# Contracting over 128 rows instead of 64 or 16 in the mixer of a two-layer decoder

## The chip, the cores and the metric

The kernel runs on one core of one Trainium2 chip. The metric is the device time of one execution in microseconds, as the median of several runs; lower is better.

## What is computed

Two decoder layers over 528 tokens (16 learned meta tokens ahead of 512) of width 1024. Each layer is a SwiGLU feed-forward network, a mixer, and a second feed-forward network, each added to a scaled residual and normalized:

```
x <- LN1(alpha*x + 0.5*SwiGLU_1(x))
x <- LN2(alpha*x + W_out [Pool(u_pool) ; GLA(q,k,v,r,g)])
x <- LN3(alpha*x + 0.5*SwiGLU_2(x))
where [u_pool | q | k | v | r | g_lowrank] = x @ W_in
```

The change is in GLA, gated linear attention with 4 heads, keys of 64 and values of 128 per head:

```
def step(S, xs):                       # one chunk of tokens, one head
    b = cumsum(gc)
    o_inter = (qc * exp(b)) @ S        # queries times the state before the chunk
    A = tril(sum_d qc[i,d] kc[j,d] exp(b[i,d] - b[j,d]))
    o_intra = A @ vc
    S_new = S * exp(b_last) + (kc * exp(b_last - b)).T @ vc
    return S_new, o_inter + o_intra
...
o = o * rsqrt(mean(o*o) + eps)         # per head and token
o = o * gla_norm_g * silu(r)
```

## The kernel before

Activations lie transposed, features on the 128 partitions and tokens in the free dimension. Weights come from HBM in pieces of 128 x 1024 float32. Each piece is split into a high part (`w_hi`, float32r) and a low part (`w_lo`, float32r), and each product is three float32r matmuls, of 264 or 512 columns: high by high, high by low, low by high (lines 442, 443 and 444 in the mixer). In the mixer ScalarE writes `w_hi` and the negated high part into `w_lo`, and POOL issues a DMA that adds the raw piece to `w_lo` (`add_raw`, L351). In parts of the feed-forward networks POOL computes `w_lo` itself (`split`, L358). POOL does these in the order of the pieces, in one loop.

Every engine follows an order written out by hand, with semaphores between them. In `mixer` TensorE runs input projections (`project`), and between them small float32 products of the attention: `diagonal`, `level(0)` to `level(6)`, transposes of values and keys, `chunk_updates` (the state increments). VectorE computes decayed queries and keys, sums the states (`states`, L1644 and L1646, tile `state`: partitions 0 to 63 hold the even head of a pair, 64 to 127 the odd one), and pools.

The products that the change touches are these:

- `attend(h)`, for head h: for each of 4 chunks of 128 tokens, values times attention matrix (`v_tok` by `acc_a`, L760, 128 rows), and for chunks 1 to 3 also the state before the chunk times the decayed queries (`state` by `qe`, L758). Both have 128 columns. Behind them come the 16 last tokens: state by queries (L762) and tail values by tail attention (`v_tail` by `acc_t`, L764), 16 columns each. L758 and L762 contract over the 64 partitions of their head, `rows(h)`; L764 contracts over 16 partitions.
- `spread_rms(h)`: four products (L791) each broadcast one row of `rms_rows` to all partitions, contracting over 16 partitions. It is called for heads 0 and 1 together and for heads 2 and 3 together.

`attend` is a generator. `beside` takes one of its matmuls after every second to fourth big matmul of `project(19)` or `pool_part(0)` to `pool_part(2)` in the first layer, and after every one or two of the second layer, whose big matmuls have 512 columns. So each small product stands alone between big ones:

```
                def beside(small, parts, every):

                    for i, m in enumerate(parts):
                        if i % every == every - 1:
                            next(small, None)
```

`mean_squares` (L777) contracts over 128 rows with 16 output rows. VectorE copies each head's result (`take_o`), multiplies by the broadcast reciprocals (`finish_o`), and the second half of the output projection follows (`gla_part`). Ahead of the mixer, the norm writes `x_hi` (ScalarE, L1053) and `x_lo` (VectorE, L1496) tile by tile; TensorE's first mixer products follow them tile by tile, the last of each tile at L433. The decayed queries `qe` are written by VectorE at L1545, and the tail values by `v_tail_copy` (L1603). `v_transpose(h)` (L694) waits for the tail copy of the head before.

Of the kernel before, what the change touches and what calls it, by code (L numbers as in the profile page):

```python
# [15 lines left out]
ALU = mybir.AluOpType  # L16
ACT = mybir.ActivationFunctionType

P = 128
D = 1024  # L20
# [99 lines left out]
def by_dma(n):  # L120

    r = n % LAYER_PIECES
    return n >= SLOTS and (r < SLOTS or FFN_PIECES <= r < FFN_PIECES + MIX_IN + MIX_OUT + SLOTS)
# [49 lines left out]
def build(nc, x_t, stream, params, out_t):  # L173
    ctx = ExitStack()
    with ctx:
        def sb(name, shape, dt=F32, where=ctx):
            return where.enter_context(nc.sbuf_tensor(name, shape, dt))
# [21 lines left out]
        rms_comb = sb("rms_comb", [P, 2 * RMS_ROWS - 1])  # L199
        rms_rows = sb("rms_rows", [RMS_ROWS, T // QUARTERS])  # L200
        ident = sb("ident", [P, P])
# [8 lines left out]
        acc_a = sb("acc_a", [P, HEADS, NCH, CH])  # L210
        acc_t = sb("acc_t", [META, HEADS, META])

# [34 lines left out]
        kdec = sb("kdec", [P, 2, SEQ])  # L247
        qe = sb("qe", [P, 2, T])
        elast = sb("elast", [P, 2, NCH])
        ft = sb("ft", [P, 2, T])  # L250
        win = sb("win", [P, 2, T])
        v_tok = sb("v_tok", [P, HEADS, NCH, DV])
        v_tail = sb("v_tail", [META, HEADS, DV])
        kd_tok = sb("kd_tok", [P, 2, NCH, CH])
# [26 lines left out]
        def matmul_parts(ps, span):  # L281
# [15 lines left out]
            u_acc s_step s_done pool_step pool_done wsplit_step o_acc o_done osq_done ms_acc rms_std rms_inv rms_spread o_scaled o_fin  # L297
            o_hi_done o_lo_done acc_zero
            p1_acc p5_acc p6_acc p7_acc p3_acc p1_copied p5_copied u2_copied c22_done c12_done
# [46 lines left out]
        def _(pool):  # L346
# [24 lines left out]
            for i, s in enumerate(LEVELS):  # L371
# [9 lines left out]
                pool.wait_ge(S["consts"], n)  # L381
            nc.gpsimd.memset(acc_t[:, :, :], 0.0).then_inc(S["masks"], 1)
            for n in range(SLOTS, DEPTH * LAYER_PIECES):
                if by_dma(n):
                    add_raw(n)
                elif whole(n):
                    split(n)
# [8 lines left out]
        def _(pe):  # L396
# [209 lines left out]
            def mixer(l, span):  # L606
# [49 lines left out]
                def rows(h):  # L656
                    return slice((h % 2) * DK, (h % 2 + 1) * DK)
# [89 lines left out]
                def attend(h):  # L747

                    ps = 2 + h % 2
                    if h < 2:  # L750
                        pe.wait_ge(S["lev_evac"], l * 7 + 7)
                        pe.wait_ge(S["s_done"], l * 2 + 2)
                    else:
                        pe.wait_ge(S["o_done"], l * 4 + (h - 1))
                    for c in range(NCH):
                        tok = slice(c * CH, (c + 1) * CH)
                        if c > 0:
                            yield nc.tensor.matmul(PS[ps][:, 0, tok], state[rows(h), h // 2, c - 1, :], qe[rows(h), h // 2, tok],  # L758
                                                   start=True, stop=False, skip_group_check=True)
                        yield nc.tensor.matmul(PS[ps][:, 0, tok], v_tok[:, h, c, :], acc_a[:, place(h), c, :], start=c == 0,  # L760
                                               stop=True, skip_group_check=True)
                    yield nc.tensor.matmul(PS[ps][:, 1, 0:META], state[rows(h), h // 2, NCH - 1, :], qe[rows(h), h // 2, TAIL:T],  # L762
                                           start=True, stop=False, skip_group_check=True)
                    yield nc.tensor.matmul(PS[ps][:, 1, 0:META], v_tail[:, h, :], acc_t[:, place(h), :], start=False,  # L764
                                           stop=True, skip_group_check=True).then_inc(S["o_acc"], 1)
# [16 lines left out]
                def spread_rms(h):  # L782

                    pe.wait_ge(S["masks"], 1)
                    pe.wait_ge(S["rms_inv"], l + 1)
                    if h >= 2:
                        pe.wait_ge(S["o_scaled"], l * 4 + (h - 1))
                    for q in range(QUARTERS):
                        row = h * QUARTERS + q
                        bank, at = divmod(q * n_quarter, span[1])  # L790
                        m = nc.tensor.matmul(PS[2 + h % 2][:, bank, at:at + n_quarter],  # L791
                                             ident[0:RMS_ROWS, row:row + 1].to_broadcast([RMS_ROWS, P]),
                                             rms_rows[:, 0:n_quarter], start=True, stop=True)
                    m.then_inc(S["rms_spread"], 1)
# [97 lines left out]
        def _(act):  # L892
# [177 lines left out]
            def mixer(l, span):  # L1070
# [78 lines left out]
                def o_high(h):  # L1149
# [5 lines left out]
                n_quarter = (T - span[0]) // QUARTERS  # L1155
                nc.scalar.activation(rms_rows[:, 0:n_quarter], PS[2][0:RMS_ROWS, 0, 0:n_quarter], ACT.Sqrt,
                                     bias=rms_eps[0:RMS_ROWS, :]).then_inc(S["rms_std"], 1)
# [41 lines left out]
        def _(dve):  # L1199
# [308 lines left out]
            def mixer(l, span):  # L1508
# [35 lines left out]
                V.tensor_copy(elast[:, :, :], chunks(pair_exp[0])[:, :, :, CH - 1])  # L1544
                V.tensor_tensor(qe[:, :, :], qk[:, 0:2, :], pair_exp[0], ALU.mult).then_inc(S["qe_done"], 1)  # L1545
                dve.wait_ge(S["qe_done"], l + 1)

# [29 lines left out]
                def take_level(i):  # L1577
# [12 lines left out]
                    if s <= META // 2:  # L1590
                        x.then_inc(S["arg_step"], 1)
                        nb = META // 2 // s
                        dst = acc_t[:, :, :].rearrange("p h (b i) -> p h b i", i=2 * s)[:, :, :, s:2 * s]
                        src = PS[3][0:META, 0, 0:32].rearrange("p (g b i) -> p g b i", b=nb, i=s)
                        msk = level_mask[0:META, i, 0:META // 2].rearrange("p (o b i) -> p o b i", o=1, i=s)\
                            .to_broadcast([META, HEADS, nb, s])
                        x = V.copy_predicated(dst, msk, src)
# [3 lines left out]
                def v_tail_copy(h):  # L1601
                    dve.wait_ge(S["vtr_acc"], l * 4 + (h + 1))
                    V.tensor_copy(v_tail[:, h, :], PS[3][0:META, 0, 256:256 + DV]).then_inc(S["v_tail_done"], 1)  # L1603

# [75 lines left out]
                for hp in range(2):  # L1680
# [13 lines left out]
                dve.wait_ge(S["tdiag_acc"], l + 1)  # L1694
                V.copy_predicated(acc_t[:, :, :], ident_mask[0:META, 0:META].rearrange("p (o i) -> p o i", o=1)
                                  .to_broadcast([META, HEADS, META]),
# [40 lines left out]
                n_quarter = (T - span[0]) // QUARTERS  # L1737
                V.reciprocal(rms_rows[:, 0:n_quarter], rms_rows[:, 0:n_quarter]).then_inc(S["rms_inv"], 1)
                take_pool_part(4)
# [13 lines left out]

            for ap, val in ((ones_mean[:, :], 1.0 / D), (ones[:, :], 1.0), (rms_comb[:, :], 0.0), (chunk_mask[:, :], 1.0),
                            (warm[:, :], 1.0), (rms_eps[:, :], RMS_EPS)):
                i = V.memset(ap, val)
# [96 lines left out]
```

## Time and profile before

| what | value |
|---|---|
| median of 3 runs | 1888.67 us (1888.56 to 1888.8) |
| the profiled execution | 1891.47 us, of which 1889.7 us span |
| TensorE matmul busy | 1856.0 us (98%), 14406 instructions |
| VectorE busy | 1181.7 us (63%) |
| ScalarE busy | 882.0 us (47%) |
| POOL busy | 348.4 us (18%) |
| mean granted TensorE clock | 0.989 of full |
| HBM traffic | 108 GB/s over the span |

The span is the time from the first to the last instruction; the execution's own time has 1.8 us more around it. A float32 matmul is two records in the trace, so `xN` counts twice the products of the code there. A matmul's duration is modelled and overlaps its neighbours', so what an instruction costs is read from the distance between starts, not from its duration. In `64*128` the first number is the rows over which a matmul contracts, the second the output rows.

### The profile page before, as it was taken

What the parts mean: (1) busy time and instruction counts of PE and PEld (TensorE: products, weight loads), DVE (VectorE), ACT (ScalarE), POOL (GpSimd) and SP (SyncE); (2) the same over time, 40 slices, a digit from 0 to 9 for tenths busy, and PEclk for the clock granted to TensorE, in tenths of its full rate; (3) what the DMA queues carried; (4) which work ended last, traced back from release to release, by engine and by line L of the source; (5) the groups of instructions that cost most, each with busy time, mean ns of one, the idle gap of its engine ahead of it and who ended that gap; (6) DMA issues with size and microseconds to landing.
All of it is one profiled execution on the core that took longest, in us unless ns stands there. A gap on an engine that the chain in (4) does not pass through costs nothing.

```text
span 1889.7 us, 34669 instructions
## 1 busy us (share of the span) xinstructions
PE 1856.0 (98%) x14406; PEld 1774.5 (94%) x14406; DVE 1181.7 (63%) x1834; ACT 882.0 (47%) x1357; POOL 348.4 (18%) x200
## 2 busy tenths in 40 slices
PE   8999999999999999999999999999999999999997
PEld 8999999999899999999999999999997779899895
DVE  5728637568447827728487286476683478286475
ACT  4524525474336534525465254255742465255253
POOL 3030210410001140130420302104100120402113
PEclk9999999999998999999999999999999999999998
DMA  4323322556444332333533333225655543233232
GB/s 157 101 90 113 112 81 99 157 134 134 105 103 96 101 112 90 102 92 101 143 101 103 92 108 113 90 95 152 143 126 112 112 95 106 89 112 115 87 113 90
DMA packets 57469, 206.73 MB, mean 109 GB/s; under 512 B 6368, under 2 KB 6368, under 8 KB 57312
## 3 DMA queue, kind: packets, MB, share of 16 engines
q1 hardware_dynamic: 48240, 171.78, 29.1%
q0 software_dynamic: 8640, 31.46, 9.0%
q8 instruction: 115, 1.88, 0.4%
q10 hardware_dynamic: 432, 1.25, 0.2%
q14 instruction: 42, 0.34, 0.1%
HBM read 202.38 MB, written 2.10 MB: 108 GB/s over the span
## 4 chain that ended last, share of the span: by engine, by line
PE 96%; DVE 2%; ACT 1%; issue 0%; DMA 0%; ACTq 0%; DVEq 0%
PE PS L462 13%; PE PS L465 13%; PE PS L464 13%; PE PS L401 9%; PE PS L402 9%; PE PS L403 9%; PE PS L442 6%; PE PS L443 6%; PE PS L444 6%; PE PS L411 2%; PE PS L433 2%; PE PS L412 2%; PE PS L727 1%; PE PS L562 1%; PE PS L758 1%; DVE h_lo L1208 0%
## 5 line engine op out<-in xcount | busy, mean ns | idle before, releaser
L358 POOL TENSOR_TENSOR w_lo<-raw,w_hi 128x1024 fp32r<-128x1024 f32 x112 | 284.0, 2541 | 1083.7 <-ACT w_hi L916 1057.3
L401 PE MATMUL PS<-h_hi,w_hi 128*128 128x264 f32 (+1 forms) x1238 | 370.2, 299 | 0.5 <-DVE h_lo L1208 0.3
L402 PE MATMUL PS<-h_lo,w_hi 128*128 128x264 f32 (+1 forms) x1238 | 369.7, 299 | 0.0
L403 PE MATMUL PS<-h_hi,w_lo 128*128 128x264 f32 (+1 forms) x1238 | 369.4, 298 | 0.0
L916 ACT ACTIVATE w_hi<-raw 128x1024 fp32r<-128x1024 f32 x240 | 215.1, 930 | 233.0 <-PE PS L403 179.3
L462 PE MATMUL PS<-v_hi,s_hi 128*128 128x264 f32 (+1 forms) x864 | 244.8, 283 | 0.1
L464 PE MATMUL PS<-v_lo,s_hi 128*128 128x264 f32 (+1 forms) x864 | 244.3, 283 | 0.0
L465 PE MATMUL PS<-v_hi,s_lo 128*128 128x264 f32 (+1 forms) x864 | 243.9, 282 | 0.0
L401 PEld LDWEIGHTS PS<-h_hi,w_hi 128*128 128x128 f32 x1238 | 233.0, 188 | 9.2 <-DVE h_lo L1208 1.6
L402 PEld LDWEIGHTS PS<-h_lo,w_hi 128*128 128x128 f32 x1238 | 233.1, 188 | 7.4
L403 PEld LDWEIGHTS PS<-h_hi,w_lo 128*128 128x128 f32 x1238 | 232.3, 188 | 7.3
L910 ACT ACTIVATE s_hi<-s_sum 128x512 fp32r<-128x512 f32 x288 | 178.1, 631 | 100.8 <-PE PS L465 96.7
L442 PE MATMUL PS<-x_hi,w_hi 128*128 128x264 f32 (+1 forms) x696 | 208.2, 299 | 1.7 <-ACT s_r L1143 1.6
L443 PE MATMUL PS<-x_lo,w_hi 128*128 128x264 f32 (+1 forms) x696 | 205.9, 296 | 0.0
L444 PE MATMUL PS<-x_hi,w_lo 128*128 128x264 f32 (+1 forms) x696 | 205.6, 295 | 0.0
L1274 DVE TENSOR_TENSOR s_lo<-s_sum,s_hi 128x512 fp32r<-128x512 f32 x288 | 190.5, 687 | 18.5 <-ACT s_hi L910 17.8
L465 PE MATMUL PS<-x_hi,w_lo 128*128 128x264 f32 (+1 forms) x576 | 163.1, 283 | 0.0
L464 PEld LDWEIGHTS PS<-v_lo,s_hi 128*128 128x128 f32 x864 | 162.9, 188 | 0.0
L462 PEld LDWEIGHTS PS<-v_hi,s_hi 128*128 128x128 f32 x864 | 162.5, 188 | 0.3 <-ACT PS L957 0.3
L462 PE MATMUL PS<-x_hi,w_hi 128*128 128x264 f32 (+1 forms) x576 | 162.7, 282 | 0.0
L465 PEld LDWEIGHTS PS<-v_hi,s_lo 128*128 128x128 f32 x864 | 162.4, 188 | 0.0
L464 PE MATMUL PS<-x_lo,w_hi 128*128 128x264 f32 (+1 forms) x576 | 161.5, 280 | 0.0
(226 smaller groups left out, 4112.4 us busy)
## 6 DMA issues: line engine op xcount, KB each, us to landing
raw<-in_stream SPq DMA_DIRECT2D x316, 512.0 KB, 3.7
w_lo<-in_stream POOLq DMA_DIRECT2D x60, 512.0 KB, 7.7
raw_first<-in_stream SPq DMA_DIRECT2D x4, 512.0 KB, 5.7
out_t<-X SPq DMA_DIRECT2D x8, 256.0 KB, 2.1
X<-in_x_t SPq DMA_DIRECT2D x7, 264.0 KB, 7.3
par<-in_params ACTq DMA_DIRECT2D x2, 480.0 KB, 3.4
X<-in_x_t ACTq DMA_DIRECT2D x1, 264.0 KB, 4.6
```

What stands on the lines that cost most here:

```text
L358: nc.gpsimd.tensor_tensor(w_lo[:, slot, :], raw[:, slot % RAWS, :], w_hi[:, slot, :].bitcast(F32), ALU.subtract).then_inc(lo_done[slot], 1)
L401: nc.tensor.matmul(o, hi, rhs_hi[:, k, tok], start=first, stop=False)
L402: nc.tensor.matmul(o, hi, rhs_lo[:, k, tok], start=False, stop=False)
L403: return nc.tensor.matmul(o, lo, rhs_hi[:, k, tok], start=False, stop=last)
L442: yield nc.tensor.matmul(o, hi, rhs_hi[:, k, tok], start=k == 0, stop=False)
L443: yield nc.tensor.matmul(o, hi, rhs_lo[:, k, tok], start=False, stop=False)
L444: yield nc.tensor.matmul(o, lo, rhs_hi[:, k, tok], start=False, stop=k == n - 1)
L462: nc.tensor.matmul(o, hi[:, w], rhs_hi[:, k, :], start=start and k == 0, stop=False, skip_group_check=True)
L464: nc.tensor.matmul(o, hi[:, w], rhs_lo[:, k, :], start=False, stop=False, skip_group_check=True)
L465: m = nc.tensor.matmul(o, lo[:, w], rhs_hi[:, k, :], start=False, stop=stop and k == BAND - 1, skip_group_check=True)
L916: nc.scalar.activation(w_hi[:, n % SLOTS, part], raw[:, n % RAWS, part], ACT.Copy).then_inc(S["raw_hi"], 1)
L1274: V.tensor_tensor(s_lo[:, j - 1, :], s_sum[:, j - 1, :], s_hi[:, j - 1, :].bitcast(F32), ALU.subtract).then_inc(S["s_lo_done"], 1)
```

## The change

`qe` gets a further dimension for the parity of the head. Each half holds one head's decayed queries in its 64 partitions and zeros in the other 64, so that L758 and L762 contract over all 128 partitions of `state`; the foreign state is multiplied by zero. `v_tail`, `acc_t` and `rms_rows` grow to 128 partitions with zeros below the 16 that carry data, and L764 and L791 contract over 128. VectorE writes `qe` in two operations of 64 partitions. POOL writes the zeros of `qe` and `v_tail` once per layer (`pad`), ahead of its fifth addition in the mixer and behind a wait for the norm's last `x_hi`. `v_tail_copy` and `attend` wait for them. The zeros of `acc_t` come from the memset that was there, of `rms_rows` from one more memset at the start. The number and the order of TensorE's instructions stay.

```diff
-        rms_rows = sb("rms_rows", [RMS_ROWS, T // QUARTERS])
+        rms_rows = sb("rms_rows", [P, T // QUARTERS])
...
-        acc_t = sb("acc_t", [META, HEADS, META])
+        acc_t = sb("acc_t", [P, HEADS, META])
...
-        qe = sb("qe", [P, 2, T])
+        qe = sb("qe", [P, 2, 2, T])
...
-        v_tail = sb("v_tail", [META, HEADS, DV])
+        v_tail = sb("v_tail", [P, HEADS, DV])
...
+            def pad(l):
+
+                pool.wait_ge(S["x_hi_done"], (l * LN_PER + 1) * KC + KC)
+                nc.gpsimd.memset(qe[DK:P, 0, :, :], 0.0).then_inc(S["padded"], 1)
+                nc.gpsimd.memset(qe[0:DK, 1, :, :], 0.0).then_inc(S["padded"], 1)
+                pool.wait_ge(S["padded"], l * 3 + 2)
+                nc.gpsimd.memset(v_tail[:, :, :], 0.0).then_inc(S["padded"], 1)
+
             for n in range(SLOTS, DEPTH * LAYER_PIECES):
+                if n % LAYER_PIECES == FFN_PIECES + SLOTS:
+                    pad(n // LAYER_PIECES)
...
                         pe.wait_ge(S["s_done"], l * 2 + 2)
+                        pe.wait_ge(S["padded"], l * 3 + 3)
...
-                            yield nc.tensor.matmul(PS[ps][:, 0, tok], state[rows(h), h // 2, c - 1, :], qe[rows(h), h // 2, tok],
+                            yield nc.tensor.matmul(PS[ps][:, 0, tok], state[:, h // 2, c - 1, :], qe[:, h % 2, h // 2, tok],
                                                    start=True, stop=False, skip_group_check=True)
...
-                    yield nc.tensor.matmul(PS[ps][:, 1, 0:META], state[rows(h), h // 2, NCH - 1, :], qe[rows(h), h // 2, TAIL:T],
+                    yield nc.tensor.matmul(PS[ps][:, 1, 0:META], state[:, h // 2, NCH - 1, :], qe[:, h % 2, h // 2, TAIL:T],
...
-                                             ident[0:RMS_ROWS, row:row + 1].to_broadcast([RMS_ROWS, P]),
+                                             ident[:, row:row + 1].to_broadcast([P, P]),
                                              rms_rows[:, 0:n_quarter], start=True, stop=True)
...
-                nc.scalar.activation(rms_rows[:, 0:n_quarter], PS[2][0:RMS_ROWS, 0, 0:n_quarter], ACT.Sqrt,
+                nc.scalar.activation(rms_rows[0:RMS_ROWS, 0:n_quarter], PS[2][0:RMS_ROWS, 0, 0:n_quarter], ACT.Sqrt,
...
-                V.tensor_tensor(qe[:, :, :], qk[:, 0:2, :], pair_exp[0], ALU.mult).then_inc(S["qe_done"], 1)
-                dve.wait_ge(S["qe_done"], l + 1)
+                V.tensor_tensor(qe[0:DK, 0, :, :], qk[0:DK, 0:2, :], ex[0:DK, 0:2, :], ALU.mult).then_inc(S["qe_done"], 1)
+                V.tensor_tensor(qe[DK:P, 1, :, :], qk[DK:P, 0:2, :], ex[DK:P, 0:2, :], ALU.mult).then_inc(S["qe_done"], 1)
+                dve.wait_ge(S["qe_done"], l * 2 + 2)
...
                     dve.wait_ge(S["vtr_acc"], l * 4 + (h + 1))
-                    V.tensor_copy(v_tail[:, h, :], PS[3][0:META, 0, 256:256 + DV]).then_inc(S["v_tail_done"], 1)
+                    dve.wait_ge(S["padded"], l * 3 + 3)
+                    V.tensor_copy(v_tail[0:META, h, :], PS[3][0:META, 0, 256:256 + DV]).then_inc(S["v_tail_done"], 1)
...
-            for ap, val in ((ones_mean[:, :], 1.0 / D), (ones[:, :], 1.0), (rms_comb[:, :], 0.0), (chunk_mask[:, :], 1.0),
+            for ap, val in ((ones_mean[:, :], 1.0 / D), (ones[:, :], 1.0), (rms_comb[:, :], 0.0), (rms_rows[:, :], 0.0), (chunk_mask[:, :], 1.0),
                             (warm[:, :], 1.0), (rms_eps[:, :], RMS_EPS)):
```

The remaining hunks restrict operations on `acc_t` and `rms_rows` to the 16 partitions that they had.

The order on POOL, from the end of the setup on. `add_raw` is the row `DMA w_lo<-in_stream`. Before:

```order
26 L382 MEMSET acc_t 16x64
27 L358 TENSOR_TENSOR w_lo<-raw,w_hi 128x1024 x28
28 L351 DMA w_lo<-in_stream 128x1024 x28
29 L358 TENSOR_TENSOR w_lo<-raw,w_hi 128x1024 x28
```

With the change:

```order
26 L382 MEMSET acc_t 128x64
27 L358 TENSOR_TENSOR w_lo<-raw,w_hi 128x1024 x28
28 L351 DMA w_lo<-in_stream 128x1024 x4
29 L386 MEMSET qe 64x1056
30 L387 MEMSET qe 64x1056
31 L389 MEMSET v_tail 128x512
32 L351 DMA w_lo<-in_stream 128x1024 x24
33 L358 TENSOR_TENSOR w_lo<-raw,w_hi 128x1024 x28
```

Three memsets now stand between the fourth and the fifth of the 28 additions of the first layer's mixer; the second layer's has the same.

The order on VectorE in the mixer, around the writing of `qe`. Before:

```order
327 L1540 TENSOR_TENSOR ex<-bcum 128x512 x2
328 L1544 COPY elast<-ex 128x8
329 L1545 TENSOR_TENSOR qe<-qk,ex 128x1056
330 L1681 COPY_PREDICATED acc_a<-ident_mask,PS 128x1024 x2
331 L1557 TENSOR_TENSOR ex<-bcum 128x4x64
```

With the change:

```order
328 L1551 TENSOR_TENSOR ex<-bcum 128x512 x2
329 L1555 COPY elast<-ex 128x8
330 L1556 TENSOR_TENSOR qe<-qk,ex 64x1056
331 L1557 TENSOR_TENSOR qe<-qk,ex 64x1056
332 L1694 COPY_PREDICATED acc_a<-ident_mask,PS 128x1024 x2
333 L1569 TENSOR_TENSOR ex<-bcum 128x4x64
```

One operation became two, each as long in the free dimension as the one before; all behind them in the mixer stand one place later.

## Rows read from the trace of the kernel before

**Rows 1.** The page, chain of work that ended last, share of the span by engine

```profile
PE 96%; DVE 2%; ACT 1%; issue 0%; DMA 0%; ACTq 0%; DVEq 0%
```

**Rows 2.** Groups by form, TensorE: line, operation, tiles, shapes, count, busy us, mean ns

```profile
L758 PE MATMUL PS<-qe,state 64*128 64x128 f32 x48 | 11.7, 323 | 0.0
...
L791 PE MATMUL PS<-rms_rows,ident 16*128 16x132 f32 x32 | 4.1, 277 | 0.0
...
L762 PE MATMUL PS<-qe,state 64*128 64x16 f32 x16 | 3.1, 270 | 0.0
L764 PE MATMUL PS<-acc_t,v_tail 16*128 16x16 f32 x16 | 3.1, 268 | 0.0
```

**Rows 3.** Timeline, TensorE, first layer: start us, us, engine, line, operation

```profile
503.96 0.28 PE L443 MATMUL PS<-x_lo,w_hi 128*128 128x264 f32 x1
504.17 0.48 PE L758 MATMUL PS<-qe,state 64*128 64x128 f32 x2
504.59 0.39 PE L444 MATMUL PS<-x_hi,w_lo 128*128 128x264 f32 x1
504.81 0.29 PE L442 MATMUL PS<-x_hi,w_hi 128*128 128x264 f32 x1
...
505.06 0.28 PE L444 MATMUL PS<-x_hi,w_lo 128*128 128x264 f32 x1
505.18 0.38 PE L760 MATMUL PS<-acc_a,v_tok 128*128 128x128 f32 x2
...
505.53 0.28 PE L443 MATMUL PS<-x_lo,w_hi 128*128 128x264 f32 x1
```

**Rows 4.** Timeline, TensorE, a 16-column product in the same stage

```profile
509.38 0.28 PE L443 MATMUL PS<-x_lo,w_hi 128*128 128x264 f32 x1
509.60 0.39 PE L762 MATMUL PS<-qe,state 64*128 64x16 f32 x2
...
510.14 0.28 PE L442 MATMUL PS<-x_hi,w_hi 128*128 128x264 f32 x1
```

**Rows 5.** Timeline, TensorE, head sums and reciprocal broadcast of the first layer

```profile
535.52 3.77 PE L777 MATMUL PS<-ex,rms_comb 128*16 128x132 f32 x32
...
542.12 0.28 PE L444 MATMUL PS<-yp_hi,w_lo 128*128 128x264 f32 x1
542.33 2.06 PE L791 MATMUL PS<-rms_rows,ident 16*128 16x132 f32 x16
...
544.55 0.29 PE L443 MATMUL PS<-yp_lo,w_hi 128*128 128x264 f32 x1
```

**Rows 6.** Timeline, VectorE and TensorE, first mixer

```profile
415.34 1.25 DVE L1545 TENSOR_TENSOR qe<-qk,ex 128x1056 f32<-128x1056 f32 x1
...
429.56 0.27 DVE L1603 COPY v_tail<-PS 16x128 f32<-16x128 f32 x1
...
430.82 0.44 PE L694 MATMUL PS<-ident,ft 128*128 128x128 f32 x2
```

**Rows 7.** Timeline, end of the norm ahead of the first mixer

```profile
390.27 0.83 ACT L1053 ACTIVATE x_hi<-xhat,par 128x528 fp32r<-128x528 f32 x1 [0.43 <-DVE xhat L1445]
...
391.85 0.71 DVE L1496 TENSOR_TENSOR x_lo<-X,x_hi 128x528 fp32r<-128x528 f32 x1 [1.00 <-ACT X L1053]
...
392.95 0.28 PE L433 MATMUL PS<-x_lo,w_hi 128*128 128x264 f32 x1
```

**Rows 8.** One line, VectorE's h_lo: count, duration ns min/median/max, first and last start

```profile
L1208 DVE TENSOR_TENSOR h_lo<-prod,h_hi x88: 684/704/2253, 33.2 to 1840.9; 128x528 fp32r<-128x528 f32 x66, 128x512 fp32r<-128x512 f32 x22
```

**Rows 9.** Timeline, POOL, start of the program and first mixer

```profile
0.81 0.47 POOL L362 MEMSET level_mask<- 128x448 int32 x1 [0.29 <-POOLq L1846]
...
396.69 0.85 POOL L351 DMA_DIRECT2D w_lo<-in_stream  x1 [16.75 <-ACT w_lo L922]
```

**Rows 10.** Stretches of 26 us, both norms of layer one: busy by engine, clock, DMA

```profile
370.00:396.00 26.00, 24.03 (x178) 21.57 (x177) 20.26 (x38) 18.36 (x27) 1.21 (x2) 0.93 0.41 92
574.00:600.00 26.00, 24.85 (x164) 22.67 (x164) 21.20 (x41) 17.20 (x26) 1.70 (x2) 0.80 0.47 99
```

More of the change, by code:

```diff
@@ L297, in build @@
             u_acc s_step s_done pool_step pool_done wsplit_step o_acc o_done osq_done ms_acc rms_std rms_inv rms_spread o_scaled o_fin
-            o_hi_done o_lo_done acc_zero
+            o_hi_done o_lo_done acc_zero padded
             p1_acc p5_acc p6_acc p7_acc p3_acc p1_copied p5_copied u2_copied c22_done c12_done
@@ L1592, in take_level @@
                         nb = META // 2 // s
-                        dst = acc_t[:, :, :].rearrange("p h (b i) -> p h b i", i=2 * s)[:, :, :, s:2 * s]
+                        dst = acc_t[0:META, :, :].rearrange("p h (b i) -> p h b i", i=2 * s)[:, :, :, s:2 * s]
                         src = PS[3][0:META, 0, 0:32].rearrange("p (g b i) -> p g b i", b=nb, i=s)
@@ L1694, in mixer @@
                 dve.wait_ge(S["tdiag_acc"], l + 1)
-                V.copy_predicated(acc_t[:, :, :], ident_mask[0:META, 0:META].rearrange("p (o i) -> p o i", o=1)
+                V.copy_predicated(acc_t[0:META, :, :], ident_mask[0:META, 0:META].rearrange("p (o i) -> p o i", o=1)
                                   .to_broadcast([META, HEADS, META]),
@@ L1737, in mixer @@
                 n_quarter = (T - span[0]) // QUARTERS
-                V.reciprocal(rms_rows[:, 0:n_quarter], rms_rows[:, 0:n_quarter]).then_inc(S["rms_inv"], 1)
+                V.reciprocal(rms_rows[0:RMS_ROWS, 0:n_quarter], rms_rows[0:RMS_ROWS, 0:n_quarter]).then_inc(S["rms_inv"], 1)
                 take_pool_part(4)
```

## Prediction

> **What bounds the kernel.** First the chain of work that ended last: 96% of it is TensorE [rows 1], so what counts is how fast TensorE gets through its own list. Whatever shortens a gap between two of its matmuls shortens the program, unless another engine then comes late. The second view is the groups by form, which gives the counts: 48 records of the product of state and queries (24 products in the code), 16 records each of the two 16-column products, and the reciprocal broadcasts [rows 2]. Their mean durations, 268 to 323 ns, say little, since durations overlap. The third view decides: the timeline of the stage in which these products stand between big ones, read by starts.
>
> **What a 64-row product costs now.** Big products with 264 columns follow each other every 0.12 us. Around a 64-row product the starts are 503.96, 504.17, 504.59, 504.81 [rows 3]: 0.85 us from the big product before it to the second big one behind it, where two steps of 0.12 would be 0.24. The price is 0.61 us. Around a product of the same 128 columns over 128 rows the starts are 505.06, 505.18, 505.53 [rows 3]: 0.47 us, a price of 0.23. The form is the same float32 product of 128 columns, in the same stage and between the same neighbours; only the contracted rows differ. The difference of 0.38 us lies in the gap ahead (0.21 against 0.12) and above all in the gap behind (0.42 from its start to the next big start).
>
 The trace shows the narrow products with the longer gaps on both sides.
>
> **The terms of the gain.**
>
> - State by queries, 128 columns: 24 products by 0.38 = 9.1 us. I take the first layer's price for both.
> - The two 16-column products: from 509.38 to 510.14 [rows 4] is 0.76, less 0.24 is 0.52 us. There is no 16-column product over 128 rows in the trace. At worst it costs the 0.52 of now; at best the halves of the float32 product cost no more than a step of a big one, less than 0.23. I take 0.23, the price of the 128-column product, because the weight load of 128 columns stays whatever the moving side has. The saving is 0.29, for 16 products 4.6 us. The tail values contract over 16 rows and not 64, with the same mean duration [rows 2]; I give them the same price.
> - Reciprocal broadcasts: a run of 16 records with the products around it takes from 542.12 to 544.55 [rows 5], 2.43 less 0.24 = 2.19 us. For full rows: the first product 0.23 and 14 further records at 0.113 each, a step from the head sums (3.77 less a last duration of 0.27, over 31) [rows 5], make 1.81. The saving is 0.38 per run, about what one 64-row product costs more, as a gap paid once per run would have it. There are two runs in each layer: 1.5 us. The bounds are 0 and 1.5.
>
> Sum of the gain: 15.2 us. The second wait that TensorE gets ahead of `attend` is for zeros written 100 us earlier, and it already waits there for VectorE's states, so it costs nothing.
>
> **The terms of the loss.**
>
> - VectorE writes `qe` in two operations. One of 128 partitions takes 1.25 us [rows 6]; with half the partitions and the same free length I take the same duration each, some 1.15 us more behind one another. (Bounds: nothing more if half the partitions took half the time, 1.25 at most.) VectorE runs without a pause from there to the first tail copy, at 429.56 for 0.27 us [rows 6]. The second transpose of values on TensorE, at 430.82 [rows 6], waits for that copy: now it is done 0.99 us early, then 0.16 us late. With the hand-over I take 0.2 us per layer, 0.4 in all (0 to 0.6). Everything behind it has more room: VectorE next waits for TensorE's level 0.
> - POOL writes the zeros when the norm's last `x_hi` is there, at 390.27 + 0.83 = 391.10 [rows 7]. A memset of 448 elements takes 0.47 us [rows 9], 1.05 ns an element; two of 1056 and one of 512 make 2.8 us. Before, POOL stood idle for 16.75 us up to 396.69 [rows 9], waiting for ScalarE. So the zeros lie in 5.6 us of idle time, and the additions keep their place. If that cover were gone, the addition of the fifth piece would start later by the excess, and behind it the projection that uses the piece.
> - The same memsets run beside VectorE's last `x_lo`, at 391.85 for 0.71 us, which TensorE uses at 392.95 [rows 7], 0.39 us after its end. One VectorE form, `h_lo`, has a median of 704 ns and a maximum of 2253 [rows 8]. At that maximum `x_lo` would end 1.54 us later and cost 1.15 us per layer; undisturbed it costs nothing. I take 0.15 per layer, 0.3 in all, near the undisturbed end, since a memset reads nothing.
>
> The Trainium skill, GPSIMD Engine Reference, Specifications, says that POOL shares its SBUF interfaces with VectorE and that instructions with two SBUF inputs contend. `x_lo` is one. Taken at its word for memsets too it would bring the loss to the upper end; only the trace after can show it.
>
> **The clock.** In the norms the granted clock falls from 2.4 to 1.2 GHz, after TensorE has run with gaps. In 26 us around the first norm the mean is 0.93, 3.6 us at half clock, with 178 matmuls; around the second it is 0.80, 10.4 us at half clock, with 164 matmuls [rows 10]. So 6.8 us more of half clock came with 14 matmuls fewer, at 0.12 us 1.7 us of time. The change moves all work behind the first `attend` to an earlier moment, so the falls can last longer or shorter. The fall at 574 to 600 is the long one of the two and has more room to shrink than to grow; I put 0.7 us of gain for it, somewhat under half of that step, and keep 1.7 us a step on either side for the range.
>
> **Sum.** 15.2 - 0.4 - 0.3 + 0.7 = 15.2 us. The profiled execution took 1891.47 us, with a span of 1889.7; it would become 1876.3, with a span of 1874.5. The profiled execution stands 2.8 us over the median, so the median becomes 1888.67 - 15.2 = 1873.5 us.
>
> **The rivals.**
>
> 1. *Only part of the gap goes* (say the gap behind shrinks by half because something of it belongs to state or PSUM, or the 16-column and 16-row forms keep their price). Against it: the product over 128 rows writes the same PSUM bank from the same stage and has neither gap. For it: no wide product with 16 columns is in the trace. The gain is about half, 7.7 us: 1881.0 us. Chance 0.07.
> 2. *The rows are not the cause*, and state and queries cost 0.61 us over 128 rows too. Then only the losses stay, 0.7 us: 1889.4 us, no difference that can be told. Against it speaks that three forms with different operands, 64 and 16 rows, show the same extra. Chance 0.05.
> 3. *Wide products lose an overlap that narrow ones have.* As a mechanism here, each of the 40 isolated products would load its weights in the open, two steps of about 0.11 more: 8.8 us plus the 0.7 of losses, 1898.2 us. This is what the rule of TensorE: Matmul & The Clock Gate would give. Against it: the wide product in rows 3 is followed by the usual step after 0.35 us, the narrow one after 0.64. Chance 0.01.
> 4. *Slower by POOL's queue.* The memsets stand ahead of 24 additions, in the one queue that brings the low parts. They decide once they last over the 5.6 us of cover; each us above it can make each layer's projections wait up to 1 us. To end 3.8 us slower, with a gain of 14.8 to be eaten first, each layer has to lose 9.3 us: memsets of 15 us in sum, 5.7 ns an element against the 1.05 of the row. At 6.5 ns an element they take 17 us, 11.5 too long in each layer: 1888.7 - 14.8 + 23 = 1896.9 us. A memset on half the partitions, begun at partition 64, is in no row, which is what speaks for it. Chance 0.03.
>
> That the change does nothing by itself is excluded by the order: the products are there, wider, in the same places.
>
> **How the numbers follow.** The forecast has 0.84. About 0.2%, 3.8 us, is what a measurement of this kernel can tell from no change. Faster by more than that are the forecast and nearly all of rival 1: 0.91. Within it are rival 2 and what is left of rival 1: 0.05. Slower: rivals 3 and 4, 0.04. The low end is the full gain without losses and two steps of clock won: 1873.5 - 0.7 - 2.7 = 1870.1, so 1870. The high end takes the upper bound of the `x_lo` loss (2.0 more), no clock gain and one step lost (2.4), which is 1877.9, and reaches towards rival 1: 1880.
>
> **What would show it.** In the profile after: the starts around the state product like those of rows 3's wide product (0.12 and 0.35 instead of 0.21 and 0.64); a run of broadcasts of 2.05 us between its neighbours and not 2.43; `qe` twice at about 1.25 us; a new wait of TensorE for the `v_tail` copy of 0.1 to 0.3 us; POOL's memsets between 391 and 394 us, and the first addition behind them still at about 397. `x_lo` at over 1 us beside the memsets would show the contention. The prediction is wrong if the state product keeps a gap of over 0.4 us behind it, if the additions move, or if the stretches at 1.2 GHz change by more than 7 us in sum.

## Result and profile after

| | before | after |
|---|---|---|
| median, us (runs) | 1889.38 (6) | 1876.37 (6) |
| lowest to highest, us | 1888.56 to 1890.76 | 1875.79 to 1881.83 |
| ratio, 95% interval | | 0.9936 [0.9923, 0.9948] |
| profiled execution, us | 1891.47 | 1878.16 |
| its span, us | 1889.7 | 1876.4 |
| mean granted clock | 0.989 | 0.991 |

The changed kernel is 12.1 us faster by the ratio (1889.38 x 0.0064; the interval reaches from 9.8 to 14.5). The medians lie 13.0 us apart; the ratio is that of the means, 1877.4 and 1889.6, and the one run of 1881.83 draws it towards 1. The forecast was 15.2 us less and 1873.5 us. The sign and the range held; the middle was some 2 to 3 us too hopeful. The profiled executions differ by 13.3 us.

Lines of the changed kernel's file are 10 to 13 higher than before in this part. The page of the changed kernel, the chain of work that ended last (it answers to [rows 1]):

```profile
PE 90%; DVE 5%; ACT 2%; DMA 1%; issue 1%; ACTq 0%; DVEq 0%
```

TensorE is still the bound, busy for 98% of the span as before. It shares the chain with more of the others than its 96% before (the repeat below has 92%); a share of the chain is not yet a loss. The groups by form of the changed kernel (line, engine, operation, tile, shapes, count, busy us, mean ns, idle before; they answer to [rows 2]):

```profile
L769 PE MATMUL PS<-qe,state 128*128 128x128 f32 x48 | 9.2, 273 | 0.0
...
L802 PE MATMUL PS<-rms_rows,ident 128*128 128x132 f32 x32 | 3.9, 276 | 0.0
...
L775 PE MATMUL PS<-acc_t,v_tail 128*128 128x16 f32 x16 | 2.3, 221 | 0.0
L773 PE MATMUL PS<-qe,state 128*128 128x16 f32 x16 | 2.3, 220 | 0.0
```

The four forms together are busy for 17.7 us and were for 22.0. If only busy time were read, the change would be worth 4.3 us. What counts is the distance between starts. The timeline of TensorE with the changed kernel, around a state product, a 16-column product and a run of broadcasts (start us, duration us, engine, line, operation; they answer to [rows 3], [rows 4] and [rows 5]):

```profile
505.65 0.28 PE L453 MATMUL PS<-x_lo,w_hi 128*128 128x264 f32 x1
505.77 0.38 PE L769 MATMUL PS<-qe,state 128*128 128x128 f32 x2
...
506.12 0.28 PE L452 MATMUL PS<-x_hi,w_hi 128*128 128x264 f32 x1
...
509.90 0.28 PE L453 MATMUL PS<-x_lo,w_hi 128*128 128x264 f32 x1
510.02 0.29 PE L773 MATMUL PS<-qe,state 128*128 128x16 f32 x2
...
510.37 0.28 PE L452 MATMUL PS<-x_hi,w_hi 128*128 128x264 f32 x1
...
536.82 0.28 PE L454 MATMUL PS<-yp_hi,w_lo 128*128 128x264 f32 x1
536.94 1.96 PE L802 MATMUL PS<-rms_rows,ident 128*128 128x132 f32 x16
...
538.86 0.28 PE L453 MATMUL PS<-yp_lo,w_hi 128*128 128x264 f32 x1
```

Read as in the prediction, big start to second big start less two steps of 0.12:

| | before | forecast | after |
|---|---|---|---|
| state product, 128 columns | 0.61 | 0.23 | 506.12 - 505.65 - 0.24 = 0.23 |
| 16-column product | 0.52 | 0.23 | 510.37 - 509.90 - 0.24 = 0.23 |
| run of broadcasts | 2.19 | 1.81 | 538.86 - 536.82 - 0.24 = 1.80 |

Now the whole stage, from the first product in it to the big product behind its last run of broadcasts, in both layers. Before:

```profile
503.30 0.46 PE L760 MATMUL PS<-acc_a,v_tok 128*128 128x128 f32 x2 [0.94 <-DVE state L1646]
...
549.42 0.39 PE L442 MATMUL PS<-yp_hi,w_hi 128*128 128x264 f32 x1
...
1445.44 0.46 PE L760 MATMUL PS<-acc_a,v_tok 128*128 128x128 f32 x2 [0.95 <-DVE state L1646]
...
1490.46 0.50 PE L442 MATMUL PS<-yp_hi,w_hi 128*128 128x512 f32 x1
```

The same four in the changed kernel:

```profile
504.99 0.46 PE L771 MATMUL PS<-acc_a,v_tok 128*128 128x128 f32 x2 [0.90 <-issue]
...
543.36 0.37 PE L452 MATMUL PS<-yp_hi,w_hi 128*128 128x264 f32 x1
...
1439.84 0.46 PE L771 MATMUL PS<-acc_a,v_tok 128*128 128x128 f32 x2 [0.91 <-issue]
...
1477.05 0.48 PE L452 MATMUL PS<-yp_hi,w_hi 128*128 128x512 f32 x1
```

The stage took 46.12 and 45.02 us and takes 38.37 and 37.21: 7.75 and 7.81 less, 15.6 us in sum, where the terms of the gain had 15.2. So the gain arrived in full where it was expected, and 2.3 us of it were lost elsewhere in this profile: 503.30 against 504.99 says that 1.7 us were already lost ahead of the first such stage. The new wait at this place reads "issue" where it was VectorE; its length is unchanged (0.94 and 0.90).

Of what TensorE waits for in the changed kernel, three waits of over 0.3 us are new: once 1.1 us for VectorE's L1337 (at 1794.99), once 0.8 us for the weight stream (at 947.95), and this one (what, for what: us in total, times, longest):

```profile
PE PS L704 <- DVE v_tail L1616: 0.7, 2, 0.4
```

It is the foreseen one. Its place in the timeline of the changed kernel, VectorE and TensorE in the first mixer (it answers to [rows 6]):

```profile
416.64 1.24 DVE L1556 TENSOR_TENSOR qe<-qk,ex 64x1056 f32<-64x1056 f32 x1
417.92 1.26 DVE L1557 TENSOR_TENSOR qe<-qk,ex 64x1056 f32<-64x1056 f32 x1
...
432.14 0.27 DVE L1616 COPY v_tail<-PS 16x128 f32<-16x128 f32 x1
432.56 0.63 PE L704 MATMUL PS<-ident,ft 128*128 128x128 f32 x4 [0.36 <-DVE v_tail L1616]
```

Half the partitions take the full 1.24 us. The second operation starts 1.28 us behind the first, not 1.15, and TensorE stands for 0.36 us. The zeros, in the timeline of the changed kernel at the end of the norm (it answers to [rows 7] and [rows 9]):

```profile
392.45 0.98 POOL L386 MEMSET qe<- 64x1056 f32 x1 [11.21 <-ACT x_hi L1064]
...
393.14 0.71 DVE L1507 TENSOR_TENSOR x_lo<-X,x_hi 128x528 fp32r<-128x528 f32 x1 [1.00 <-ACT X L1064]
...
394.51 0.53 POOL L389 MEMSET v_tail<- 128x512 f32 x1
...
398.00 0.84 POOL L351 DMA_DIRECT2D w_lo<-in_stream  x1 [2.95 <-ACT w_lo L933]
```

The memsets take 2.6 us (forecast 2.8). The addition behind them is released by ScalarE, as before, after 2.95 us of idle time. `x_lo` beside the first two memsets takes 0.71 us, exactly as alone.

### The profile page after: what moved, and what is told of

Same layout as the page of the kernel before. It is cut to its first block, busy times and chain, and to the rows that moved or that the text cites. A ratio compares the mean times of both kernels' runs of the same rounds, so it can differ in the third digit from the quotient of the medians.

```text
span 1876.4 us, 34684 instructions
## 1 busy us (share of the span) xinstructions
PE 1838.4 (98%) x14406; PEld 1768.9 (94%) x14406; DVE 1179.2 (63%) x1837; ACT 881.3 (47%) x1357; POOL 351.7 (19%) x206
## 3 DMA queue, kind: packets, MB, share of 16 engines
q10 hardware_dynamic: 432, 1.25, 0.2%
## 4 chain that ended last, share of the span: by engine, by line
PE 90%; DVE 5%; ACT 2%; DMA 1%; issue 1%; ACTq 0%; DVEq 0%
PE PS L472 12%; PE PS L475 12%; PE PS L474 12%; PE PS L411 9%; PE PS L412 9%; PE PS L413 9%; PE PS L452 5%; PE PS L453 5%; PE PS L454 5%; PE PS L443 2%; PE PS L421 2%; PE PS L422 2%; PE PS L737 1%; DMA raw<-in_stream 1%; ACT X L1064 1%
## 5 line engine op out<-in xcount | busy, mean ns | idle before, releaser
L1285 DVE TENSOR_TENSOR s_lo<-s_sum,s_hi 128x512 fp32r<-128x512 f32 x288 | 190.3, 686 | 16.5 <-ACT s_hi L921 15.9
```

Of the source, the lines that this page charges most:

```text
L1285: V.tensor_tensor(s_lo[:, j - 1, :], s_sum[:, j - 1, :], s_hi[:, j - 1, :].bitcast(F32), ALU.subtract).then_inc(S["s_lo_done"], 1)
```

## Experiments

Two theories of the gain: the price of 0.38 us belongs to the change of row count (**rows**), or to something else that the change did in the same stroke (**other**: the new layout of `qe`, the place of the writes). Two of what was lost: fixed prices of the padding, or things that vary from one execution to the next. All ratios are against the kernel before, run on the same chip: its median was 1890.39 us beside the repeat, padding alone, the first run of narrow products and the earlier tail copy, and 1890.74 us beside the other four.

**The changed kernel once more**, no edit.

> The changed kernel again, beside the kernel before on one chip, to see how far its time and its clock repeat. Theory A (the gain is 15.7 us in the two attention stages, the rest is clock and weight stream): 12 to 15 us under the kernel before; the prices in the stage the same to 0.02 us (state product 0.23, 16-column product 0.23, broadcast run about 1.85), while the 1.2 GHz stretches of the norms and the waits for DMA may differ from the first profile. Theory B (the 1.6 us missing from the sum are a fixed cost of the change, such as the memsets): every profile shows the start of the first attend 1.7 us later than before.

Measured: 1876.68 us, ratio 0.9929 [0.9916, 0.9941], 13.4 us less, within the 12 to 15 of theory A; the profiled execution has a span of 1874.5 us, 15.2 less than that of before. The wait for `v_tail` is there with the same 0.7 us; the waits for the weight stream and for VectorE's L1337 are not. The first product of the attention stage starts early again:

```profile
503.22 0.46 PE L771 MATMUL PS<-acc_a,v_tok 128*128 128x128 f32 x2 [0.90 <-issue]
```

That is 503.22 against 503.30 before, so theory B is refuted. Of the 1.7 us by which the first profile was late here, the 0.4 for `v_tail` is fixed. The rest was that execution's own, and the rows of the norm ahead of the mixer say where it arose: the kernel before, from the norm's first sums to the last product of `x_hi` with `w_rank`,

```profile
370.09 0.56 PE L562 MATMUL PS<-ones_mean,sum_x 128*88 128x1 f32 x6
...
393.68 0.29 PE L616 MATMUL PS<-x_hi,w_rank 128*32 128x264 f32 x1
```

and the first profile of the changed kernel, with its 26 us around this norm (window; us, then busy time of PE, PEld, DVE, ACT, POOL with counts; granted clock, DMA share, GB/s; it answers to the first line of [rows 10]):

```profile
370.47 0.56 PE L572 MATMUL PS<-ones_mean,sum_x 128*88 128x1 f32 x6
...
394.98 0.28 PE L626 MATMUL PS<-x_hi,w_rank 128*32 128x264 f32 x1
...
370.00:396.00 26.00, 24.45 (x170) 21.54 (x169) 19.71 (x37) 17.16 (x26) 4.07 (x5) 0.87 0.43 98
```

0.38 us were lost before the norm began, and the norm took 24.51 instead of 23.59 us, 0.92 more, at a granted clock of 0.87 instead of 0.93. The repeat has 0.93 and 23.59 there, as before.

**Padding alone.** All tiles, zeros, waits and both `qe` operations of the change, but every product contracts over its old rows:

```diff
-yield nc.tensor.matmul(PS[ps][:, 0, tok], state[:, h // 2, c - 1, :], qe[:, h % 2, h // 2, tok],
+yield nc.tensor.matmul(PS[ps][:, 0, tok], state[rows(h), h // 2, c - 1, :], qe[rows(h), h % 2, h // 2, tok],
```

and the same for the 16-column products and the broadcasts.

> All of the change but the wide products: the layout of qe, the memsets, the two VectorE operations and the waits stay, and TensorE contracts over 64 and 16 rows as before. Theory A: no gain, the loss alone: 0.8 us over the kernel before (0.4 us of waiting for the v_tail copy in each layer), within 1.5 us either way for the clock; state product back at 0.61. Rival (part of the gain comes from the new layout or the shifted VectorE work, not from the rows): 3 us or more under the kernel before.

Measured: 1892.59 us, ratio 1.0010 [1.0002, 1.0019], 1.9 us slower than before. The timeline of this kernel around a state product:

```profile
505.62 0.28 PE L452 MATMUL PS<-x_hi,w_hi 128*128 128x264 f32 x1
505.83 0.49 PE L769 MATMUL PS<-qe,state 64*128 64x128 f32 x2
...
506.47 0.29 PE L454 MATMUL PS<-x_hi,w_lo 128*128 128x264 f32 x1
```

0.85 - 0.24 = 0.61 us, the old price, with the new layout. That refutes **other**. Between this kernel and the changed one only the contracted rows differ, and they stand 15.9 us apart in the medians of one chip (1892.59 - 1876.68), 15.6 in the stages. The padding by itself costs 1.9 us (0.4 to 3.6). Waits of 0.7 us for `v_tail` are part of it, and they are all that the two mixers lose. At the first mixer's start the last product of `x_hi` with `w_rank` stands at 393.13 against 393.68 before, and behind the wait the product that waits for `s_r` at 483.31 against 483.41. From there on the distance stays to 0.12 us: the first product of the next norm starts at 579.15 against 579.37, and in the second layer it is 1427.63 against 1426.04 and 1520.78 against 1519.27. What else differs between the two profiles lies in the norms and in single waits of the feed-forward networks, where executions of one kernel differ too. So the traces show a fixed price of 0.7 to 0.8 us, as was expected for this run; whether the padding costs more, the interval leaves open.

**One run of narrow products.** From the kernel before: the three state products of a head and its 16-column state product are issued without a big product between them. Each still contracts over 64 rows.

```diff
+for c in range(1, NCH):
+    tok = slice(c * CH, (c + 1) * CH)
+    nc.tensor.matmul(PS[ps][:, 0, tok], state[rows(h), h // 2, c - 1, :], qe[rows(h), h // 2, tok],
+                     start=True, stop=False, skip_group_check=True)
 yield nc.tensor.matmul(PS[ps][:, 1, 0:META], state[rows(h), h // 2, NCH - 1, :], qe[rows(h), h // 2, TAIL:T],
                        start=True, stop=False, skip_group_check=True)
```

In this form terms are missing from the output, by the start flags (the next run differs in them alone and has every term); which terms, no run says. All products are issued.

> The kernel before, with the three state products and the 16-column state product of a head issued in one run between two big matmuls instead of one by one; all stay at 64 rows. Theory A (the gap is paid when the number of rows changes, once on the way in and back): the run of four costs 4 x 0.23 + 0.38 = 1.30 us against 3 x 0.61 + 0.52 = 2.35 now, so 1.05 us less for each of 8 heads: 8.4 us under the kernel before. Rival (each product over 64 rows is slower by itself, for instance because of how its weights load): a run of about 2.3 us and no difference.

Measured: 1882.75 us, ratio 0.9959 [0.9945, 0.9972]. The four products cost 1.19 us together, where apart they cost 3 x 0.61 + 0.52 = 2.35. That is theory A; the rival expected 2.3 us and no difference.

**The same run with other start flags**, `start=c == 1` for the state products and `start=False` for the value products, so that every term is in the output.

> The kernel before with the 64-row products of a head in one run, as in the run before it, with the flags that start an accumulation set on the first product of the bank alone, so that every term is in the output. Same instructions in the same order, so both theories expect the time of the other grouped kernel, about 0.996 of the kernel before, and 1.19 us for a run of four (less two steps of 0.12).

Measured: 1883.89 us, ratio 0.9956 [0.9941, 0.9971]. The timeline of this kernel:

```profile
512.48 0.28 PE L443 MATMUL PS<-yp_lo,w_hi 128*128 128x264 f32 x1
512.69 0.93 PE L757 MATMUL PS<-qe,state 64*128 64x128 f32 x6
513.46 0.29 PE L759 MATMUL PS<-qe,state 64*128 64x16 f32 x2
...
513.91 0.28 PE L442 MATMUL PS<-yp_hi,w_hi 128*128 128x264 f32 x1
```

1.43 - 0.24 = 1.19 us for four, 0.30 each. Four wide ones would cost 3 x 0.23 + 0.23 = 0.92. So a narrow product is not dear; going into narrow rows and out of them is, once per run: 1.19 - 0.92 = 0.27 us here, where the last of the run has 16 columns and the saving of such a one alone is 0.29. Eight runs save 8 x 1.16 = 9.3 us by the stage and 8.3 (5.5 to 11.2) by the runs. It needs no padding, but stays behind the change, which pays for no switch at these products.

**Only the 16-row products widened**: tail values and broadcasts as in the change, `qe` and its products as before.

```diff
-    ident[0:RMS_ROWS, row:row + 1].to_broadcast([RMS_ROWS, P]),
+    ident[:, row:row + 1].to_broadcast([P, P]),
     rms_rows[:, 0:n_quarter], start=True, stop=True)
```

(with zeros in `rms_rows`, `v_tail` and `acc_t`, which the tail product reads over 128 partitions)

> Half of the change: tail values (16 products over 16 rows) and reciprocal broadcasts over 128 rows; states and queries stay at 64 rows, qe is one VectorE operation, POOL writes only the zeros of v_tail. Theory A: 8 x 0.29 for the tails and 4 x 0.38 for the broadcasts, 3.8 us under the kernel before, within 1.5 us for the clock; no wait for the v_tail copy. Rival (the gap goes only where both neighbours and all products of a head are wide, or the gain came from the state products alone): under 1.5 us.

Measured: 1888.05 us, ratio 0.9984 [0.9975, 0.9993], 3.0 us less (1.3 to 4.7), where theory A had 3.8 and the rival under 1.5. The timeline of this kernel:

```profile
510.36 0.28 PE L450 MATMUL PS<-x_lo,w_hi 128*128 128x264 f32 x1
510.58 0.39 PE L770 MATMUL PS<-qe,state 64*128 64x16 f32 x2
...
511.37 0.28 PE L451 MATMUL PS<-x_hi,w_lo 128*128 128x264 f32 x1
511.49 0.29 PE L772 MATMUL PS<-acc_t,v_tail 128*128 128x16 f32 x2
...
511.84 0.28 PE L450 MATMUL PS<-x_lo,w_hi 128*128 128x264 f32 x1
```

In one kernel, one microsecond apart, the 64-row product starts 0.22 us behind its neighbour and the wide one 0.12; the second big product behind the wide one starts 0.35 us after it. `qe` is one operation here, and no wait for `v_tail` is in the profile: it comes from the second `qe` operation.

**The tail copy earlier.** On the changed kernel, VectorE's fourth set of arguments goes behind the evacuation of the tail and the first `v_tail` copy.

```diff
                 decayed(1)
-                arguments(3)
                 dve.wait_ge(S["masks"], 1)
...
                 v_tail_copy(0)
+                arguments(3)
```

> The changed kernel, with the tail diagonal's evacuation and the first v_tail copy of VectorE ahead of the arguments of level 3 instead of behind them. Theory A: the copy ends about 1.1 us earlier, the wait of 0.4 us of TensorE in each layer is gone, 0.8 us under the changed kernel (ratio to the kernel before about 0.0004 lower). Rival (the wait hides another one of the same length behind it, for the token-major values or for level 1): TensorE waits at the same place or at the next level for another producer, and the time stays.

Measured: 1876.78 us, ratio 0.9929 [0.9917, 0.9942].

The copy now starts at 428.52 and takes 0.27 us; the product that waited for it starts at 429.88. The copy ends 1.09 us ahead of the product, the wait is gone in both layers, and none stands in its place. The medians did not show the 0.8 us that was expected, 1876.68 and 1876.78; they cannot tell so little.

**The same, and the gate's logits over 128 rows** (`glr` padded once with zeros; 8 products over 32 rows before).

```diff
-    par[0:2 * RANK, C_GU + t * P:C_GU + (t + 1) * P],
+    par[:, C_GU + t * P:C_GU + (t + 1) * P],
     glr[:, half * HALF:(half + 1) * HALF], start=True, stop=True)
```

> The changed kernel with the early tail copy, and with the gate logits (eight records a layer over 32 rows between big products) over 128 rows too, zeros in the rest. Theory A: one gap less per layer, 0.38 x 2 = 0.8 us, and 0.8 us for the tail copy: 1.5 us under the changed kernel, about 0.9915 to 0.992 of the kernel before. Rival (what is saved ahead of the first attend is given back, because the projections then wait for weights or for VectorE's chain of b): a new wait of TensorE before level 0 and no difference from the changed kernel.

Measured: 1875.78 us, ratio 0.9918 [0.9904, 0.9932], the best of all, but its interval overlaps that of the changed kernel. The run of gate products in the timeline of this kernel (before, the same three products started at 399.90, 400.12 and 402.31):

```profile
400.43 0.28 PE L454 MATMUL PS<-x_hi,w_lo 128*128 128x264 f32 x1
...
402.45 0.28 PE L453 MATMUL PS<-x_lo,w_hi 128*128 128x264 f32 x1
```

In the first layer 402.31 - 399.90 = 2.41 us became 402.45 - 400.43 = 2.02, 0.39 less: the switch costs the same for 32 rows as for 64 and 16.

**Six times the memsets of `qe`**, to measure POOL's cover (rival 4).

```diff
+for r in range(6):
     nc.gpsimd.memset(qe[DK:P, 0, :, :], 0.0).then_inc(S["padded"], 1)
     nc.gpsimd.memset(qe[0:DK, 1, :, :], 0.0).then_inc(S["padded"], 1)
```

> The changed kernel with the two memsets of qe written six times over: 12.9 us of memsets in each layer instead of 2.5, against 5.5 us between the norm's last x_hi and the next addition. Theory A (cover of 5.5 us, then some 4 us more because the transfer lands before its projection starts): the fifth addition starts 7.3 us late, TensorE waits 3 to 4 us for it in each layer, 6 to 8 us over the changed kernel. Rival of the prediction's fourth (every us beyond the cover is paid in full): 15 us over it. Beside the memsets, VectorE's operations with two SBUF inputs keep their duration if memsets do not contend; if they do, those from the mixer's start are longer.

Measured: 1883.08 us, ratio 0.9954 [0.9937, 0.9971]; the span of its profiled execution is 1877.6 us, 3.1 over that of the repeat. The timeline of this kernel, POOL and TensorE:

```profile
392.02 0.97 POOL L387 MEMSET qe<- 64x1056 f32 x1 [11.21 <-ACT x_hi L1065]
404.87 2.61 POOL L351 DMA_DIRECT2D w_lo<-in_stream  x3
...
410.70 0.39 PE L453 MATMUL PS<-x_hi,w_hi 128*128 128x264 f32 x1 [1.67 <-DMA w_lo<-in_stream]
```

The addition starts 12.85 us behind the start of the first memset (404.87 - 392.02), in the changed kernel 5.55 (398.00 - 392.45). It is 7.3 us later, yet TensorE waits only 1.67 us for the weights, and 2.2 in the second layer (3.9 in sum). So behind the 5.6 us of POOL's own idle time the queue has another 5.6 us (7.3 - 1.67), in the second layer 5.1, before TensorE feels it. That is less of a wait than either side expected: 3 to 4 us a layer by theory A, all 7.3 by the rival. The ratios show a loss of 4.7 us against the repeat (0.0025 of 1890), with intervals that overlap, under the 6 to 8 us expected and in agreement with the 3.9 us of waits. `x_lo` beside the memsets takes 0.71 us here too.

## Why the prediction was right, and where it was off

**The terms of the gain were right, in mechanism and size.** 15.2 us forecast, 15.6 by the stages, 15.9 by the medians with and without wide rows. Each of the three prices came out within 0.01 us. The one without a row of its own, the 16-column product over 128 rows, is 0.23, so taking the price of the 128-column product for it was right, and rival 1 (only part of the gap goes) is refuted. Giving the tail values' products over 16 rows the saving of those over 64 was right too: around the first of them the starts go from 510.39 to 511.15 before and from 510.61 to 511.09 after, which makes 0.52 and 0.24 us.

**Rival 2** (the rows are not the cause) fell with padding alone. **Rival 3** is refuted by the rows above: the second big product behind a wide one starts 0.35 us after it, as in [rows 3]. This is where the rule of the Trainium skill, TensorE: Matmul & The Clock Gate, Part 3, was set against the trace: a load of other rows could hide behind a running matmul, and narrow products would be the better ones. Here the narrow products had the gaps, 0.09 us more ahead (0.21 - 0.12) and 0.29 more behind (0.64 - 0.35, both from [rows 3]), and the wide ones have none, so for these isolated products the measurement decides against it. The page speaks of rows that differ, and the 64 rows here are part of their neighbours' 128, so what the trace refutes is this use of the rule and not the rule itself.

**Rival 4** (POOL's queue) needed memsets above 5 ns an element. They take 0.93 (0.98 us for 1056), also where they begin at partition 64. The six-fold memsets show that even its point of decision was too near: there are some 5 us more of cover than the prediction counted.

**One loss was under-sized.** The prediction had 0.7 us in sum; padding alone measures 1.9 (0.4 to 3.6), of which the traces place 0.7 to 0.8. By its steps:

- The `v_tail` wait: 0.2 per layer forecast, 0.36 measured, 0.7 in two waits, which is outside the stated bounds of 0 to 0.6. The second `qe` operation costs 1.28 us and not 1.15. The 1.15 had no row; in the trace before, the next operation starts 1.28 us behind that of `qe` (416.62 - 415.34). From the copy's end at 432.41 it is 0.15 us to TensorE's start.
- `x_lo` beside the memsets: 0.3 us forecast, nothing measured (0.71 us beside them, even in the six-fold version). The rule of the Trainium skill, GPSIMD Engine Reference, Specifications, on contention with instructions of two SBUF inputs does not show for a memset.
- The rest of the 1.9, some 1.2 us, stood in no term. It is within what the interval leaves uncertain, and the starts in both mixers of padding alone leave no place for it there.

**The clock term: its price held, its sign was luck.** The prediction took 1.7 us of time for 6.8 us more at 1.2 GHz, and 0.7 us of gain in the norm at 574 to 600. The price comes out of the rows. The norm ahead of the first mixer, read between the same two products as above, takes 23.6 us in five of the ten traces, those with a granted clock of 0.93 in the stretch from 370 to 396, and 24.4 to 24.5 us in the five with 0.87. That is 0.8 to 0.9 us for 3.1 us more at half clock (26 x 0.06 x 2). For a norm of the second layer the changed kernel's first profile has this stretch, and below it the product with which the norm begins and the last one ahead of the wait at 1794.99:

```profile
1502.00:1528.00 26.00, 22.44 (x114) 17.98 (x113) 22.03 (x43) 18.33 (x27) 1.70 (x2) 1.00 0.46 94
...
1505.81 0.58 PE L572 MATMUL PS<-ones_mean,sum_x 128*128 128x1 f32 x4 [0.63 <-DVE sum_x L1422]
...
1793.59 0.28 PE L475 MATMUL PS<-x_hi,s_lo 128*128 128x256 f32 x1
```

The same in its repeat, the same kernel:

```profile
1502.00:1528.00 26.00, 23.93 (x97) 18.73 (x97) 21.40 (x42) 17.32 (x25) 0.86 (x1) 0.80 0.37 82
...
1503.69 0.58 PE L572 MATMUL PS<-ones_mean,sum_x 128*128 128x1 f32 x4 [0.63 <-DVE sum_x L1422]
...
1793.18 0.28 PE L475 MATMUL PS<-x_hi,s_lo 128*128 128x256 f32 x1
```

In one execution this norm runs wholly at 2.4 GHz, in the other 10.4 of its 26 us (26 x 0.20 x 2) are at 1.2 GHz. Between the two products lie 287.78 and 289.49 us: the full clock gave 1.7 us, and TensorE still had them 280 us later. Right behind, the first profile waits 1.12 us for VectorE, which the repeat doesn't; VectorE had waited 2.76 us for a weight piece just before. That the execution with the long fall has the shorter span all the same, 1874.5 against 1876.4, is mostly this wait, the one of 0.8 us for the weight stream, the 0.9 us of the first norm and 0.8 us from before it. The clock was not varied by itself, so the price is what goes together in the traces.

The sign is another matter. The fall in the norm at 574 to 600 did shrink, from 0.80 to 0.87 in the first profile and in the repeat. But it is as short with padding alone, which has nothing of the gain, so the change did not cause it. In sum the page's mean clock puts 41.6 us of the trace before at 1.2 GHz (1889.7 x 0.011 x 2), 33.8 of the first profile after and 41.2 of the repeat. The first profile so meets one of the prediction's own signs of being wrong, a change of over 7 us, and the repeat doesn't: the falls differ between executions of one kernel by as much as the bound.

**The sum.** 15.6 - 1.9 = 13.7 us, against 13.4 measured for the repeat (11.2 to 15.9) and 12.1 for the first runs. The forecast of 15.2 is over the first by 3.1 us: up to 1.2 of it is the losses, 0.7 a clock gain that the change doesn't bring, and the rest is no more than the runs leave uncertain. That the repeat's profile has exactly the forecast span, 1874.5, is luck. The absolute time also moved because the kernel before took 1889.38 and not 1888.67 us in the runs beside it.

## What to carry over

Where TensorE is the bound, look at the starts around isolated matmuls that contract over fewer rows than their neighbours: here each visit to narrow rows cost 0.27 to 0.39 us, for 64, 32 and 16 rows alike and however many products stood in it. Why a change of the row count costs this, no run shows. Zeros in the unused rows remove it, at the price of whoever writes them, which must be idle or early; if that can't be had, issue the narrow products in one run and pay once. Busy time hides most of this (4.3 of 15.6 us), and a clock term should be kept for the range: its price can be read from a trace, but the falls vary between executions of one kernel.

## What the runs showed of the hardware

- The price of going to fewer rows and back is the same for 64, 32 and 16 rows (0.38, 0.39 and 0.39 us, an isolated product of 128 columns or a run of products of 132 and 264) and is paid once per run. Behind a product of 16 columns it is 0.29 us.
- An operation of VectorE on 64 of 128 partitions takes as long as on all (1.24 and 1.25 us for 1056 elements), and the next one starts 0.04 us behind its end.
- A start flag on a product reaches beyond its own columns. In the first run of narrow products every product with `start=True` is the first in its own columns of the bank, and yet terms were missing; with the flag on the bank's first product alone, and nothing else changed, all were there.
- The granted clock of one norm differed between 1.00 and 0.80 from one execution of the same kernel to the next, and 1.7 us of time went with it. In another norm 0.87 instead of 0.93 went with 0.8 to 0.9 us, in ten traces of ten.
